# A two-layer model: layer 1's rotation table built in the dense layer, one bias product at the start, projection steps in another order

## The chip, the cores and the metric

The kernel runs on one core of a Trainium2 chip. The metric is the device time of one execution in microseconds (us), as the median of several runs. Engines are named TensorE (PE in the rows, PEld for its weight loads), VectorE (DVE), ScalarE (ACT), GpSimd (POOL) and SyncE (SP), which issues most of the transfers.

## What is computed

A model of two layers on 256 tokens of width 1024. Each layer projects the normed rows, runs a state space mixer, a latent attention and a sparse attention side by side, adds a cross attention, and ends with a feed-forward part: dense in layer 0, eight experts in layer 1.

```python
for l in range(DEPTH):
    proj = rmsnorm(h, mix_norm[l]) @ w_in[l]
    u, cq, ckv, kr, nq, nkv, ngate = jnp.split(proj, offsets, axis=-1)
    y_ssm = ssm_mixer(u, ...)
    y_mla = mla_mixer(cq, ckv, kr, ..., cos, sin)
    y_nsa = nsa_mixer(nq, nkv, ngate, ..., rel_bias)
    h = h + concatenate([rmsnorm(y_ssm), rmsnorm(y_mla), rmsnorm(y_nsa)]) @ w_out[l]
    h = h + cross_attn(h, mem, ...)
    hn = rmsnorm(h, ffn_norm[l])
    if l % 2 == 0:
        h = h + swiglu(hn, dense_w_gate, dense_w_up, dense_w_down)
    else:
        h = h + moe_swiglu(hn, moe_router, moe_w_gate, moe_w_up, moe_w_down)
return rmsnorm(h, final_norm)
```

In the state space mixer the state of each group turns in the complex plane from token to token: `ab_r, ab_i = mag * cos(li * dt), mag * sin(li * dt)`. The sparse attention adds a bias that depends on the distance of two tokens (`rel_bias`, 32 buckets by 6 heads). The compressed keys and values of the sparse attention pass through a small network with a GELU (`nsa_compress`).

## The kernel before

All five engines run programs written out by hand, with semaphores between them. **Weights** come as chunks of 128 x 2048 (1 MB) through a ring of six slots (`ring`), loaded by SP (L1150 to L1180) as TensorE frees them. Each chunk is split into two parts for products of full precision: ScalarE rounds it into an upper half (`layer_chunk_upper`, L457, into `colu` or `upper`), VectorE subtracts it from the chunk and leaves the lower half in place (`layer_chunk_lower`, L461). Each product of TensorE is three matmuls (`split_product`, L437 to L439): upper by upper, upper by lower, lower by upper. The left side is split in the same way (`colr`, `coll`). A layer has 27 common chunks; chunks 0 to 6 are the input projections, in the order u (0), zA (1), zB (2), q0 (3), q1 (4), ck and cv (5), vs (6).

**Results** of TensorE go through five banks in turn (`ROT`). Each tile has a name in a list of jobs and an engine that drains it; TensorE waits until the tile five places before is drained (`wait_free`), and for inputs by name (`wait_drained`).

**The start** (layer 0): ScalarE issues three small transfers (the one-hot table of distances, the bias table, the layer's columns), SP the rows x, the constants and the first chunks. TensorE makes the bias table of 6 heads in six products of 128 x 384 (L1272); ScalarE drains two of them (L1616) and VectorE four (L1897) into the place of `qz`; GpSimd writes all to memory (L2338) and reads them back skewed (L2369). VectorE computes the angles (`angles`), ScalarE the exponential and the sines (`trigonometry`); VectorE sums the squares of x (L1863), GpSimd takes the power (L2323), ScalarE scales the first half of the rows (L1601) and VectorE the second (L1889); TensorE transposes (L1202).

**The rotation table** `ftab` (in `big`, 2 x 8 x 256 columns) holds the powers of the unit rotation for all 256 tokens. GpSimd builds it in eight doublings of six tensor operations each (`double`, L2323). In layer 0 they stand beside the projections, all ahead of the power for the latent norms (`power(2, 4)`); in layer 1 also beside the projections, the last two doublings behind that power. The states (`states(0)`, first VectorE operation L1860 that reads `big`) and ScalarE's copy of the rotated key (L1707), whose place the doublings use as scratch, wait for it.

**VectorE in the projections**: lower half of chunk 4, squares of the latent columns (L1863), gates (L1977), rotation of the shared key (`rotate`), lower half of chunk 5, clearing and filling of `kc` and `qz` (L1998 to L2005), lower half of chunk 6, drains, the output parameters `cp` (L1860, L2026), the drain of `vs` (L2028), the lower half of the memory's columns (L2052), then states and query rotations. The GELU of the compressed tokens (L1720) stands on ScalarE behind the drains of queries, keys and values; TensorE's products of the result are L1376 to L1378.

**The dense layer** (`dense_pe`, `dense_act`, `dense_dve`) goes over 11 pieces of 256 columns; most of it is a loop with two pieces a turn. For each piece ScalarE copies the transposed units (L757), makes the upper halves of three chunks (L480) and takes the sigmoid product (L750); VectorE makes the remainders (L886, L486, L880). GpSimd has no part in it.

## Time and profile before

| | |
|---|---|
| time, median of 3 runs | 1760.9 us (1760.01 to 1760.96) |
| profiled execution | 1759.99 us, span 1758.2 us |
| TensorE busy | 1674.5 us (95%), mean granted clock 0.983 |
| VectorE busy | 1363.7 us (78%) |
| ScalarE busy | 1081.3 us (61%) |
| GpSimd busy | 225.8 us (13%) |
| layer 0: projections to cross attention | 0 to about 290 us |
| layer 0: dense layer | about 290 to 481 us |
| layer 1: projections to cross attention | about 481 to 770 us |
| layer 1: experts | about 770 us to the end |

A row of a timeline has the start in us from the span's start, the duration, the engine with the line of the kernel, the operation, what it writes and reads, shapes and count. In brackets stands how long the engine was idle before it, and which instruction of which engine ended that. A merged row (x4) lasts from the first start to the last end. A row of a table of stretches has, after the stretch and its length, the busy time and the number of instructions of each engine, then the mean granted clock of TensorE (1.00 is full, 0.50 half), the busy share of the transfer engines and what they moved. A row of waits has the engine and line that waited, who released it, the total in us, how many times, and the longest.

### The profile page before, as it was taken

Reading aid. Unit: us, or ns where it says so; the run is one execution under the profiler, and the core shown is the slowest. Engines: PE = TensorE matmul, PEld = TensorE weight load, DVE = VectorE, ACT = ScalarE, POOL = GpSimd, SP = SyncE. Lnnn points to the kernel's source line nnn. Section 1 sums busy time; section 2 is a strip of 40 time slices with the busy share of each in tenths; the row PEclk is TensorE's granted clock in tenths of the full one; section 3 lists DMA queues with packets and bytes.
Section 4 is the critical chain, followed back from the end, with each engine's and each line's share of the span. In section 5 each row is a group of like instructions: output and inputs, shape, how many; then the busy total and the mean of one; then the engine's idle time right before and its main releaser. Section 6 shows DMA issues by size and latency. Waiting matters only on the chain.

```text
span 1758.2 us, 24308 instructions
## 1 busy us (share of the span) xinstructions
PE 1674.5 (95%) x8490; PEld 1399.4 (80%) x8490; DVE 1363.7 (78%) x1508; ACT 1081.3 (61%) x1190; POOL 225.8 (13%) x236
## 2 busy tenths in 40 slices
PE   7799999999987999989999999999999999999995
PEld 6768888888785888878888888888888888888783
DVE  6876656545568756578898989998989999889895
ACT  4355454434353554447777777777777777777773
POOL 6534001000066420031000000000000000000200
PEclk9899999999999999989999999999999999999998
DMA  9402334955431124249999999999999999999992
GB/s 369 158 24 71 146 144 151 367 189 191 174 138 48 49 96 164 102 184 422 377 377 378 376 381 375 370 389 381 375 381 376 383 377 362 388 372 357 418 364 83
DMA packets 67610, 475.94 MB, mean 271 GB/s; under 512 B 7544, under 2 KB 7544, under 8 KB 12889
## 3 DMA queue, kind: packets, MB, share of 16 engines
q1 hardware_dynamic: 62016, 450.93, 66.9%
q0 software_dynamic: 5296, 24.04, 3.5%
q8 instruction: 39, 0.64, 0.1%
q10 hardware_dynamic: 232, 0.12, 0.1%
q14 instruction: 27, 0.21, 0.0%
HBM read 461.82 MB, written 13.24 MB: 270 GB/s over the span
## 4 chain that ended last, share of the span: by engine, by line
PE 82%; DVE 9%; ACT 4%; issue 3%; DMA 2%; POOL 1%; DVEq 0%; ACTq 0%; POOLq 0%; SPq 0%
PE bank L437 24%; PE bank L439 24%; PE bank L438 24%; DVE lower L461 2%; ACT upper L480 1%; PE bank L628 1%; DMA ring<-in_weights 1%; PE bank L1423 1%; ACT upper L457 1%; DVE xel L986 1%; PE bank L1521 1%; PE bank L1313 1%; PE bank L1422 1%; DVE row L1860 1%; PE bank L1202 1%
## 5 line engine op out<-in xcount | busy, mean ns | idle before, releaser
L486 DVE TENSOR_TENSOR lower<-ring,upper 128x2048 fp32r<-128x2048 f32 x369 | 845.6, 2292 | 145.8 <-ACT upper L480 132.8
L480 ACT ACTIVATE upper<-ring 128x2048 fp32r<-128x2048 f32 x369 | 706.3, 1915 | 111.3 <-PE bank L439 101.8
L437 PE MATMUL bank<-upper,xeu 128*128 128x512 f32 x896 | 359.8, 402 | 3.9 <-DVE lower L486 3.2
L439 PE MATMUL bank<-upper,xel 128*128 128x512 f32 x896 | 350.5, 391 | 0.0
L438 PE MATMUL bank<-lower,xeu 128*128 128x512 f32 x896 | 349.5, 390 | 0.0
L437 PE MATMUL bank<-upper,htu 128*128 128x512 f32 x536 | 209.7, 391 | 5.3 <-DVE htl L1002 3.8
L439 PE MATMUL bank<-upper,htl 128*128 128x512 f32 x536 | 208.7, 389 | 0.0
L438 PE MATMUL bank<-lower,htu 128*128 128x512 f32 x536 | 208.6, 389 | 0.0
L437 PEld LDWEIGHTS bank<-upper,xeu 128*128 128x128 f32 x896 | 168.3, 188 | 36.4 <-DVE lower L486 4.4
L439 PEld LDWEIGHTS bank<-upper,xel 128*128 128x128 f32 x896 | 168.2, 188 | 35.9
L438 PEld LDWEIGHTS bank<-lower,xeu 128*128 128x128 f32 x896 | 168.7, 188 | 31.7
L461 DVE TENSOR_TENSOR lower<-ring,upper 128x2048 fp32r<-128x2048 f32 x42 | 99.3, 2364 | 67.3 <-ACT upper L457 66.9
L437 PEld LDWEIGHTS bank<-upper,htu 128*128 128x128 f32 x536 | 100.6, 188 | 31.0 <-issue 9.7
L457 ACT ACTIVATE upper<-ring 128x2048 fp32r<-128x2048 f32 x42 | 80.3, 1912 | 60.5 <-PE bank L439 60.5
L439 PEld LDWEIGHTS bank<-upper,htl 128*128 128x128 f32 x536 | 100.6, 188 | 21.1
L438 PEld LDWEIGHTS bank<-lower,htu 128*128 128x128 f32 x536 | 100.6, 188 | 20.5
L439 PE MATMUL bank<-colr,lower 128*128 128x256 f32 x384 | 110.3, 287 | 0.0
L800 ACT ACTIVATE htu<-bank 128x256 fp32r<-128x256 f32 x112 | 43.4, 388 | 98.1 <-PE bank L628 97.8
L2323 POOL TENSOR_TENSOR small<-small,cst 128x2 f32<-128x2 f32 (+2 forms) x12 | 20.3, 1690 | 570.9 <-DVE small L1866 570.8
L437 PE MATMUL bank<-colr,upper 128*128 128x256 f32 x256 | 76.1, 297 | 11.2 <-DVE lower L461 9.4
L796 ACT ACTIVATE big<-bank 128x256 f32<-128x256 f32 x112 | 43.0, 384 | 65.8 <-PE bank L439 65.8
L439 PE MATMUL bank<-upper,coll 128*128 128x512 f32 (+1 forms) x208 | 77.7, 374 | 0.0
(376 smaller groups left out, 2574.8 us busy)
## 6 DMA issues: line engine op xcount, KB each, us to landing
ring<-in_weights SPq DMA_DIRECT2D x423, 1024.0 KB, 5.7
routed_rows<-g POOLq DMA_DIRECT2D x1, 4096.0 KB, 36.6
lp<-in_lparams POOLq DMA_DIRECT2D x1, 3634.5 KB, 14.2
lp<-in_lparams SPq DMA_DIRECT2D x1, 3584.0 KB, 13.6
memraw<-routed_rows POOLq DMA_DIRECT2D x7, 512.0 KB, 6.2
expert_rows<-xk POOLq DMA_DIRECT2D x7, 512.0 KB, 6.9
skewed_bias<-attn POOLq DMA_DIRECT2D x1, 1152.0 KB, 10.9
h<-in_x SPq DMA_DIRECT2D x1, 1024.0 KB, 5.3
```

The lines of the kernel that those rows point to most:

```text
L437: pe.matmul(to, x_up, w_up, start=start, stop=False, skip_group_check=True)
L438: pe.matmul(to, x_up, w_lo, start=False, stop=False, skip_group_check=True)
L439: return pe.matmul(to, x_lo, w_up, start=False, stop=stop, skip_group_check=True)
L457: act.activation(upper_slot(c), ring[:, c % RING, :], ACT.Copy).then_inc(wt_upper[l], 1)
L461: dve.tensor_tensor(lower[:, c % RING, :], ring[:, c % RING, :], f32(upper_slot(c)), ALU.subtract).then_inc(wt_split[l], 1)
L480: act.activation(upper[:, third(q), :], ring[:, q % RING, :], ACT.Copy).then_inc(done, 1)
L486: dve.tensor_tensor(lower[:, q % RING, :], ring[:, q % RING, :], f32(upper[:, third(q), :]), ALU.subtract).then_inc(done, 1)
L628: ins = pe.transpose(banks[2][:, f * P:(f + 1) * P], hr[:, i % 2, 0, f * P:(f + 1) * P], ident)
L796: act.activation(gs[:, i % 2, 0, :], banks[i % 2][:, 0:256], ACT.Silu).then_inc(m["silu"], 1)
L800: act.activation(htu[:, i % 2, 0:256], banks[2][:, 0:256], ACT.Copy).then_inc(m["ht_up"], 1)
L986: ins = dve.scalar_tensor_tensor(xel[buf][:, k, :], banks[5 + k // 4][:, (k % 4) * P:(k % 4 + 1) * P], cols[:, C_FFN + k:C_FFN + k + 1], f ...
L2323: return pool.tensor_tensor(out, a, b, op)
```

## The change

In the program's order:

- The columns are the first of ScalarE's three transfers. TensorE makes one bias product of 6 x 384 (heads by distances); VectorE drains it into one row per head (`biasrow`, in `vm`); SP writes it to memory 128 times over, between chunk 5 and chunk 6. ScalarE's first drain of `vm` waits for that write.
- In layer 0 ScalarE sums the squares of x, and VectorE scales both halves of the rows. Layer 1 keeps the old division.
- On VectorE, in both layers, the lower half of chunk 5 stands ahead of the gates, and the key's rotation behind the lower half of chunk 6.
- On ScalarE, in both layers, the GELU stands ahead of the drains of queries, keys and values.
- On GpSimd, in layer 0, the power for the latent norms stands ahead of the last doubling.
- Layer 1's step lengths, angles and sines are computed in the dense layer, around pieces 6 and 7, which are taken out of the loop. GpSimd builds layer 1's table there, into `col` and `row`, with scratch in `g` and `big`. When TensorE has done its last product of the layer, ScalarE copies the table to `big` (two copies of 2048 columns), ahead of its scaling of the rows.
- TensorE's wait for the split memory columns moves from before the loop over the heads to its first use in it (the second turn).

```diff
-        bias = attn[:, 2 * NH * T:2 * NH * T + NH * 384].rearrange("p (h n) -> p h n", h=NH)
-        biasrows = vm[0:33, :, :].rearrange("p t n -> p (t n)")
+        biasrow = vm[0:NH, 0, :]
...
@@ dense_act @@
-            with act.Fori(1, (DENSE_PIECES - 1) // 2 - 1) as r:
+            e = (DENSE_PIECES - 1) // 2 - 2
+            with act.Fori(1, e) as r:
                 step(0, 2 * r, r)
                 step(1, 2 * r + 1, r)
+            next_steps()
+            step(0, 2 * e, e)
+            next_trigonometry()
+            step(1, 2 * e + 1, e)
...
@@ dense_dve @@
+            next_angles()
+            step(0, 2 * e, e)
+            step(1, 2 * e + 1, e)
...
@@ block.sync @@
+            sp.wait_ge(p_dve, 2)
+            sp.dma_start(scratch[:, :, :], biasrow.unsqueeze(1).broadcast_to([NH, P, 384])).then_inc(s_scr, 16)
             load(RING, RING)
...
@@ block.tensor @@
-            pe.wait_ge(p_dve, 2)
-            for hh in range(NH):
-                mm(banks[2 + hh][:, 0:384], biasrows[:, hh * P:(hh + 1) * P], pt[0:33, 0, 0:384],
-                   start=True, stop=True).then_inc(p_pe, 1)
+            pe.wait_ge(p_dve, 1)
+            mm(banks[7][0:NH, 0:384], pt[0:33, 1, 0:NH], pt[0:33, 0, 0:384], start=True, stop=True).then_inc(p_pe, 1)
...
@@ block.scalar @@
+            act.dma_start(lp[:, 0:LP["cols"][1]], lparams[0][:, 0:LP["cols"][1]]).then_inc(cols_landed, 16)
             act.dma_start(pt[0:33, 0, :], onehot).then_inc(bias_landed, 16)
             act.dma_start(pt[0:33, 1, 0:NH], relb).then_inc(bias_landed, 16)
-            act.dma_start(lp[:, 0:LP["cols"][1]], lparams[0][:, 0:LP["cols"][1]]).then_inc(cols_landed, 16)
             act.wait_ge(cols_landed, 16)
             step_lengths(0)
-            bias_drain(0)
+            act.wait_ge(x_landed, 16)
+            for t in range(TT):
+                ins = A(xkf[:, t * D:(t + 1) * D], h[:, t, :], ACT.Square, accum_out=ss[:, t:t + 1])
+            ins.then_inc(p_act, 1)
             trigonometry(0)
-            bias_drain(1)
 
             for l in range(L):
                 if l:
-                    act.wait_ge(next_lp_landed, 16)
-                scale_rows(1)
-                if l:
-                    step_lengths(l)
+                    act.wait_ge(weights_used, RING + LAYER_CHUNKS)
+                    act.wait_ge(ftab_ready[l], 1)
+                    A(bigf[:, 2048:4096], rowf, ACT.Copy).then_inc(ftab_ready[l], 1)
+                    A(bigf[:, 0:2048], colf, ACT.Copy).then_inc(ftab_ready[l], 1)
+                    act.wait_ge(ftab_ready[l], 3)
+                    scale_rows(1)
                 else:
                     layer_chunk_upper(act, 0, 0)
...
@@ block.vector @@
+            angles(0)
             dve.wait_ge(bias_landed, 32)
...
             for l in range(L):
-                norm_h(xkf, l)
...
+                if l:
+                    norm_h(xkf, l)
+                    scale_rows(1)
+                else:
+                    dve.wait_ge(p_act, 1)
+                    mean_eps(0, 2, D).then_inc(ss_ready[l], 1)
+                    dve.wait_ge(rstd_ready[l], 1)
+                    for t in range(TT):
+                        dve.tensor_scalar(row[:, t, :], h[:, t, :], rstd[:, t:t + 1], None, ALU.mult).then_inc(row_ready[l], 1)
+                    dve.wait_ge(p_pe, 1)
+                    dve.tensor_copy(biasrow, banks[7][0:NH, 0:384]).then_inc(p_dve, 1)
...
@@ block.gpsimd @@
             for l in range(L):
                 pool.wait_ge(ss_ready[l], 1)
                 power(0, 2, rstd_ready[l])
                 if l == 0:
+                    tables(0, ftab[:, 0], ftab[:, 1], kTf[:, 512:])
+                    for m in (1, 2, 4, 8, 16, 32):
+                        link(double(m))
+                    pool.wait_ge(p_dve, 3)
                     power(6, 2, p_pool)
                     link(double(64))
-                    double(128).then_inc(ftab_ready[l], 1)
                 pool.wait_ge(ss_ready[l], 2)
                 power(2, 4, rstd_ready[l])
                 if l == 0:
+                    double(128).then_inc(ftab_ready[l], 1)
...
                     pool.wait_ge(next_lp_landed, 16)
+                    tables(1, *(f.rearrange("p (j n) -> p j n", j=8) for f in (colf, rowf)), bigf[:, 3072:4096])
+                    for m in (1, 2, 4, 8, 16, 32, 64):
+                        link(double(m))
+                    double(128).then_inc(ftab_ready[1], 1)
```

VectorE in the projections of a layer, from the means of the latent squares to the lower half of chunk 6. L461 (L462 after the change) is a lower half, L1860 (L1871) on `rt` is the rotation. Before:

```order
L1866 TENSOR_SCALAR small<-small 128x2 x2
L1977 TENSOR_SCALAR small<-small 128x36
L1978 MEMSET row 128x2x64
L1860 TENSOR_TENSOR rt<-row,cst 128x32 x2
L1860 TENSOR_TENSOR row<-rt 128x2x16
L1860 TENSOR_TENSOR rt<-row,cst 128x32 x2
L1860 TENSOR_TENSOR row<-rt 128x2x16
L461 TENSOR_TENSOR lower<-ring,upper 128x2048
L1998 MEMSET attn 128x2x256
```

And with the change:

```order
L1877 TENSOR_SCALAR small<-small 128x2 x2
L462 TENSOR_TENSOR lower<-ring,upper 128x2048
L1984 TENSOR_SCALAR small<-small 128x36
L1985 MEMSET row 128x2x64
L1998 MEMSET attn 128x2x256
L1999 COPY attn<-lp 128x2x16
L2000 MEMSET attn 64x768
L2001 MEMSET attn 64x768
L2004 COPY attn<-bank 64x512
L2005 COPY attn<-bank 64x512
L462 TENSOR_TENSOR lower<-ring,colu 128x2048
L1871 TENSOR_TENSOR rt<-row,cst 128x32 x2
```

The lower half of chunk 5 stands seven operations earlier, and the rotation behind the lower half of chunk 6.

GpSimd between the layers, from its last transfer of layer 0 to layer 1's first power (on `small`, 128x2) and the table. Before:

```order
L2400 DMA expert_rows<-g 16x1x64
L2323 TENSOR_TENSOR small<-small,cst 128x2
L2341 COPY big<-small 128x8
L2342 COPY big<-small 128x8
L2323 TENSOR_TENSOR big<-big 128x8
```

And with the change, the end of the table, whose first rows now follow the transfer directly:

```order
L2325 TENSOR_TENSOR col<-col 128x8x128
L2325 TENSOR_TENSOR g<-row 128x1024
L2325 TENSOR_TENSOR row<-col,row 128x8x128
L2325 TENSOR_TENSOR big<-row,col 128x1024
L2325 TENSOR_TENSOR col<-col,g 128x8x128
L2325 TENSOR_TENSOR row<-row,big 128x8x128
L2325 TENSOR_TENSOR small<-small,cst 128x2
L2325 TENSOR_TENSOR small<-small,cst 128x4
L2325 TENSOR_TENSOR lp<-g,big 128x512 x2
```

The whole table (two copies and 48 operations) stands ahead of layer 1's first power, and nothing of it is left between the powers and the states.

## Rows read from the trace of the kernel before

**Rows 1.** Waits of TensorE, 0 to 110 us

```profile
PE bank L1376 <- ACT hidr L1721: 2.5, 1, 2.5
```

**Rows 2.** Waits of TensorE, 478 to 620 us

```profile
PE bank L1202 <- ACT row L1601: 7.3, 1, 7.3
```

**Rows 3.** Timeline of the start, all engines

```profile
1.76 0.38 ACTq L1639 DMA_DIRECT2D lp<-in_lparams  x1
...
11.19 1.22 DVE L1863 CUSTOM_DVE_ANT_0 xk<-h 128x1024 f32<-128x1024 f32 x1
...
13.92 0.69 POOL L2323 TENSOR_TENSOR small<-small,cst 128x2 f32<-128x2 f32 x1 [13.47 <-DVE small L1866]
...
20.85 0.55 PE L437 MATMUL bank<-colr,colu 128*128 128x256 f32 x1 [1.27 <-DVE coll L1873]
```

**Rows 4.** Transfers issued from 0 to 40 us: count, size, median us to landing

```profile
skewed_bias<-attn POOLq DMA_DIRECT2D x1, 1152.0 KB, 10.9
h<-in_x SPq DMA_DIRECT2D x1, 1024.0 KB, 5.3
...
lp<-in_lparams ACTq DMA_DIRECT2D x1, 50.5 KB, 7.2
```

**Rows 5.** Busy time of each engine in stretches of both layers' starts

```profile
20.00:24.00 4.00, 3.15 (x15) 3.18 (x16) 4.00 (x9) 2.31 (x3) 3.60 (x15) 1.00 1.01 410
24.00:28.00 4.00, 4.00 (x34) 4.00 (x34) 3.81 (x6) 0.00 (x0) 3.98 (x3) 1.00 0.79 329
...
488.50:491.50 3.00, 3.00 (x15) 3.00 (x15) 1.07 (x3) 2.99 (x8) 0.00 (x0) 0.50 0.00 0
491.50:492.00 0.50, 0.50 (x5) 0.50 (x4) 0.50 (x2) 0.49 (x3) 0.00 (x0) 0.68 0.00 0
```

**Rows 6.** Timelines of VectorE and TensorE, layer 0's projections, 49 to 86 us

```profile
49.59 1.29 DVE L1977 TENSOR_SCALAR small<-small 128x36 f32<-128x36 f32 x1
...
58.65 4.43 DVE L461 TENSOR_TENSOR lower<-ring,upper 128x2048 fp32r<-128x2048 f32 x1
...
63.13 0.58 PE L437 MATMUL bank<-colr,upper 128*128 128x256 f32 x1 [9.37 <-DVE lower L461]
...
68.43 2.29 DVE L461 TENSOR_TENSOR lower<-ring,colu 128x2048 fp32r<-128x2048 f32 x1
...
75.52 0.42 DVE L2026 SCALAR_TENSOR_TENSOR cp<-cp,pt 128x256 f32<-128x256 f32 x1
...
77.12 0.27 PE L1326 MATMUL bank<-cst,row 128*128 128x128 f32 x1
...
83.52 1.13 PE L1313 MATMUL bank<-uT,lp 128*128 128x256 f32 x4
...
84.69 1.29 DVE L1860 TENSOR_TENSOR lp<-bank,big 128x512 f32<-128x512 f32 x2 [0.41 <-PE bank L1313]
```

**Rows 7.** The same two engines in layer 1's projections, 540 to 548 us

```profile
540.23 2.55 DVE L2026 SCALAR_TENSOR_TENSOR cp<-cp,pt 128x256 f32<-128x256 f32 x1
...
543.56 2.07 PE L1313 MATMUL bank<-uT,lp 128*128 128x256 f32 x4 [4.17 <-DVE vs L2028]
...
547.15 1.27 DVE L1860 TENSOR_TENSOR lp<-bank,big 128x512 f32<-128x512 f32 x2
```

**Rows 8.** Timeline of GpSimd: end of layer 0's table; start and end of layer 1's

```profile
60.89 4.41 POOL L2323 TENSOR_TENSOR big<-big,attn 128x1024 f32<-128x1024 f32 x1
...
497.64 0.20 POOL L2341 COPY big<-small 128x8 f32<-128x8 f32 x1 [10.73 <-ACT small L1625]
...
539.98 2.52 POOL L2323 TENSOR_TENSOR big<-big,attn 128x1024 f32<-128x1024 f32 x1
```

**Rows 9.** The dense layer: a stretch of it, and ScalarE's timeline in one piece

```profile
428.00:473.00 45.00, 45.00 (x206) 37.24 (x205) 20.76 (x16) 17.50 (x16) 0.00 (x0) 1.00 0.51 186
...
395.30 0.60 ACT L757 ACTIVATE htu<-bank 128x512 fp32r<-128x512 f32 x1 [4.04 <-PE bank L518]
395.79 1.91 ACT L480 ACTIVATE upper<-ring 128x2048 fp32r<-128x2048 f32 x1
```

More of the change, by code:

```diff
@@ L332, in trunk @@
         s_out = sem("s_out")
+        bias_back = sem("bias_back")
         mem_kept = sem("mem_kept")
@@ L902, in dense_dve @@
             step(1, 1)
-            with dve.Fori(1, (DENSE_PIECES - 1) // 2 - 1) as r:
+            e = (DENSE_PIECES - 1) // 2 - 2
+            with dve.Fori(1, e) as r:
                 step(0, 2 * r, r)
                 step(1, 2 * r + 1, r)
+            next_angles()
+            step(0, 2 * e, e)
+            step(1, 2 * e + 1, e)
             step(DENSE_PIECES - 3, DENSE_PIECES - 3)
@@ L1611, in transposes_upper @@
                     ins.then_inc(tr_upper[l], 1)
-            def bias_drain(hh):
-                act.wait_ge(p_pe, hh + 1)
-                A(bias[:, hh, :], banks[2 + hh][:, 0:384], ACT.Copy).then_inc(p_act, 1)
             def step_lengths(l):
@@ L1894, in _ @@
                 dve.memset(ap, v)
-            def bias_drain(hh):
-                dve.wait_ge(p_pe, hh + 1)
-                dve.tensor_copy(bias[:, hh, :], banks[2 + hh][:, 0:384]).then_inc(p_dve, 1)
             q = [par[:, i, :] for i in range(16)]
@@ L1946, in _ @@
                     mean_eps(6, 2, D).then_inc(p_dve, 1)
-                else:
-                    angles(l)
                 layer_chunk_lower(dve, l, 2)
@@ L2291, in _ @@
                 if l == 0:
-                    dense_dve(dve, last_half)
+                    dense_dve(dve, last_half, lambda: angles(1))
                 else:
@@ L2329, in _, with tables, double @@
             pool.wait_ge(cst_landed, 16)
+            table = {}
+            def tables(l, re, im, other):
+                table.update(re=re, im=im, other=other)
+                pool.wait_ge(trig_ready[l], 4)
+                pool.tensor_copy(re[:, :, 0:1], par[:, 8, :].unsqueeze(2))
+                link(pool.tensor_copy(im[:, :, 0:1], par[:, 7, :].unsqueeze(2)))
+            def double(m):
+                re, im = table["re"], table["im"]
+                a, b = (f[:, :, m - 1:m].broadcast_to([P, 8, m]) for f in (re, im))
+                x = gf[:, 0:8 * m].rearrange("p (j n) -> p j n", j=8)
+                y = table["other"][:, 0:8 * m].rearrange("p (j n) -> p j n", j=8)
+                tt(re[:, :, m:2 * m], re[:, :, 0:m], a, ALU.mult)
+                tt(x, im[:, :, 0:m], b, ALU.mult)
+                tt(im[:, :, m:2 * m], re[:, :, 0:m], b, ALU.mult)
+                link(tt(y, im[:, :, 0:m], a, ALU.mult))
+                tt(re[:, :, m:2 * m], re[:, :, m:2 * m], x, ALU.subtract)
+                return tt(im[:, :, m:2 * m], im[:, :, m:2 * m], y, ALU.add)
             for l in range(L):
@@ L2368, in _ @@
                     skew = bass.AP(scratch.tensor, 127, [[383, P], [P * 384, NH], [1, T]])
-                    pool.dma_start(btab[:, :, :], skew).then_inc(s_scr, 16)
-                else:
-                    link(double(64))
-                    double(128).then_inc(ftab_ready[l], 1)
+                    pool.dma_start(btab[:, :, :], skew).then_inc(bias_back, 16)
                 for j in range(8):
```

94 lines of the change are left out of this document (31 added, 63 removed).

## The prediction

> **What bounds the kernel now.** The profiled execution lasted 1759.99 us, with a span of 1758.2; the median of the runs is 1760.9, 0.9 above it. I read the page first: TensorE is busy 95% of the span, and its row of tenths is near 9 everywhere except at the start of each layer. So only time in which TensorE stands still or runs at its low clock can be won. I then asked for TensorE's waits in the two places where the change works, and for the timelines of the other engines around them.
>
> In layer 0, TensorE waits 9.37 us in one piece for VectorE's lower half of a weight chunk [rows 6], and 2.5 us for the GELU [rows 1]. The 2.5 us come again in layer 1, with an equal row. Where layer 1 begins it waits 7.3 us for the scaled rows [rows 2]. The start is a chain of landings and small steps: the first feature product stands at 20.85 us [rows 3]. VectorE and GpSimd hold each other up: the same L2026 took 0.42 us in layer 0, with GpSimd idle [rows 6], and 2.55 us in layer 1, while GpSimd was at the last steps of its table [rows 7, 8].
>
> **The change, part by part.**
>
> *Start.* The step sizes' columns are issued third on ScalarE's queue, at 1.76 us, and land 7.2 later, at 8.96; x, the first transfer of all, takes 5.3 and is there near 6 [rows 3, 4]. VectorE's angles stand between the columns and its squares of x at 11.19; GpSimd's power follows at 13.92 [rows 3]. Now the columns are issued first, at about 0.74. With the same 7.2 they land at 7.9. ScalarE squares x at once, at about 1.2 us for each half (VectorE's row has 1.22), so the power starts near 11.0, 2.9 sooner. Scaling both halves on VectorE costs some 0.3 more than one on each engine, but the first product waits for ScalarE's half of chunk 0, and ScalarE is free 3.2 sooner, since it neither drains bias products nor scales a row. I take **3.2 us**. If the columns land no sooner it is 2.2; if they take the 5.3 us of x, another 1.9 sooner, it is 5.1. The six bias products vanish into this; the single one runs before the rows are there. The bias write moves from GpSimd's queue to SP's, behind chunk 5 and ahead of chunk 6 and the big parameter load. Its reader, the skew load, is wanted only after 100 us, and chunk 6 only near 59, so I cost it at nothing; it would cost something if it held SP's transfers for over 20 us, against the 10.9 it took before [rows 4].
>
> The clock: 15 matmuls fit between 20 and 24 us and 34 in the next four, so TensorE went from its low level to its high one at about 24 us, some 3.3 us after the first product, although it had been busy with bias products and transposes before [rows 5]; the column of the granted clock prints 1.00 for both stretches, so here the counts are read. At the start of layer 1, the level rose in the half microsecond after 491.5, right behind three in which TensorE did 15 transposes at the low level [rows 5]. The Trainium skill's "TensorE: Matmul & The Clock Gate" (Part 4) says that transposes do not count as activity for the gate. The rows of layer 1 speak against it. By the page the rise stays 3.3 us behind the first product, as it was; by layer 1's rows it may come with the first product. I take no gain, and 1.2 us as its bound: 15 products at 0.21 us against 0.13, the pace at which VectorE hands over the columns.
>
> *Layer 0, chunk halves.* From 49.59 to 58.65 VectorE does the gates and the key rotation, slowed by GpSimd; then the lower half of chunk 5, 4.43 us where an undisturbed one takes 2.29 [rows 6]. TensorE had been ready at 63.13 - 9.37 = 53.76. Put ahead, that half is done between 51.9 and 54.0: the 9.4 us wait goes. What is late next is chunk 6. TensorE needs it after 48 products, 5.6 us later, at 59.4. VectorE has the gates (1.5) and the 5.3 us of clearing and copying that stand between the two halves now (63.1 to 68.43), so that half begins near 59.8 and ends at 62.1 to 64.2: a new wait of 2.7 to 4.8 us. The products of chunk 6 then end at 67.7 to 69.8, against 77.12 before, where L1326 follows them [rows 6]: 7.3 to 9.4 won. L1313 stood 6.4 us behind that point, at 83.52 [rows 6]. The rotation, copies, parameter products and the drain of "vs" behind it end near 73 at the latest, before L1313 wants that bank (74.1 at the earliest), and GpSimd's table, which ended at 65.3 [rows 8], starts over 3 us sooner. If the new wait drops the clock, up to 2 us are lost. I take **8.0**, with ends at 5.3 and 9.4.
>
> *GELU.* It is put ahead of the drains of the query and key products; its table load fits into ScalarE's idle time before them. TensorE's 2.5 us wait goes in both layers [rows 1]. The scores behind need VectorE's drain of "kcv" and its second scan, both done by then. **5.0 us**; should half of one wait come back elsewhere, 3.7.
>
> *Layer 1's table.* GpSimd ran it from 497.64 to 542.5 [rows 8], beside the projections. Without it VectorE runs as in layer 0 after 66 us. There the scan of the first state begins 1.17 us after TensorE's L1313 (83.52 to 84.69) [rows 6]; in layer 1 L1313 waited 4.17 and VectorE came 3.59 after it, at 547.15 [rows 7]. Without both it begins at 539.39 + 1.17 = 540.56: **6.6 us**. Bound: 5.0, if the rotation behind chunk 6 costs VectorE more. Then the clock: the four matmuls of L1313 took 2.07 us at the low level and 1.13 at the high one [rows 6, 7]; two such spells follow the waits in layer 1, so I take **1.0**, between 0 and 2.
>
> *Where the table goes.* In the dense layer TensorE is busy all of the 45 us from 428 to 473, VectorE 20.8, GpSimd not at all [rows 9]. ScalarE has 4.04 us idle ahead of each piece's copy [rows 9], which hides the added exponential and sines and their table loads, and the sigmoid's reload behind them delays nothing that TensorE needs within 5 us. The lower halves may be stretched by the 2.1 us seen above; they are ready some 6 us ahead of their use, an estimate from the order of the program and 5.6 us for each chunk's products. The table starts near 428 and takes 45 us at most, since VectorE was fuller beside it in layer 1: done by 473. ScalarE's two copies of 2048 columns (1.91 each [rows 9]) fit into the 7.3 us wait [rows 2]. Cost: nothing.
>
> Sum: 3.2 + 8.0 + 5.0 + 6.6 + 1.0 = 23.8. The profiled execution would take 1736.2, a median 1737.1. The stream of weights in the experts' part is paced by TensorE and moves with it.
>
> **Rivals.**
>
> *The wait moves instead of going (22%).* In layer 0 GpSimd's longest steps still stand beside VectorE. If the clearing, the copies and chunk 6 each meet them, that half ends at 67 rather than 63, and the clock drops too: 3 us of the 8.0 remain, 18.8 in all, **1742**. For it: everything that VectorE did from 49 to 65 was stretched [rows 6]. Against: fills and reads of PSUM were not.
>
> *More is won (12%).* The columns land early, TensorE never cools in layer 1, the start warms sooner: 5.1 + 9.4 + 5.0 + 6.6 + 2.0 + 1.2 = 29.3, **1732**.
>
> *The dense layer pays (6%).* Some eight lower halves fall beside the table. If TensorE felt 2.1 us of each, 17 us would be given back: **1754**. Against it: their lead of some 6 us.
>
> *Slower (3%).* GpSimd is starved in the dense layer and layer 1 starts late. The copies must end by 487, the table thus by 483; each microsecond beyond that is lost. It must take 45 + 10 us to cost anything, and over 45 + 10 + 23.8 + 3.5 = 82 us to make the kernel slower. At 90 us, 35 late: **1772**. VectorE is half idle there, so this is remote.
>
> *Nothing that can be told (3%).* Layer 0's gain and the start's fail, and dense and expert parts give back the rest: **1760**.
>
> **The numbers.** The forecast has 54%. The range must leave out 2 in 10: from 1730 to 1748 it takes in the forecast with its bounds (2.2 + 5.3 + 3.7 + 5.0 = 16.2, so 1744.7), the first two rivals, and no more. A measurement here tells 0.2%, about 3.5 us, from no change: faster 94%, within 3%, slower 3%.
>
> **What would show it.** First product near 17.6; no 9.4 us wait, one of 3 to 5 us at chunk 6; no wait for the GELU in either layer; L1313 of layer 1 without a wait; 0.42 us in place of 2.55 for the last parameter product; GpSimd's table in the dense layer, near 414 to 459, for 14 us are won ahead of it; TensorE still full there. I would be wrong if layer 0's wait stayed near 9, or if ScalarE's copies ended after GpSimd's power at the start of layer 1.

## The result, and the profile after

The changed kernel takes **1737.7 us** (median of 4 runs, 1735.67 to 1739.33), against 1760.5 for the kernel before in the same comparison: a ratio of 0.988, 95% interval 0.9861 to 0.9898. Faster by 1.2%, and 0.7 us from the forecast of 1737. The profiled execution took 1737.24 us, with a span of 1735.3, 22.9 less than before (the sum of the prediction's terms was 23.8).

| | before | after |
|---|---|---|
| span of the profiled execution | 1758.2 us | 1735.3 us |
| TensorE busy | 1674.5 us (95%) | 1664.6 us (96%) |
| first feature product | 20.85 us | 15.45 us |
| first transposes of the latents behind chunk 6, layer 0 | 77.12 us | 68.66 us |
| first scores of layer 0 | 108.99 us | 98.47 us |
| first transposes of layer 1 | 488.29 us | 477.86 us |
| first state's products of layer 1 | 543.56 us | 528.32 us |
| first scores of layer 1 | 573.64 us | 551.72 us |

Up to the first scores of layer 0, 10.5 us are won; from there to the start of layer 1 nothing (379.4 us now, 379.3 before); from there to layer 1's first scores 11.5; behind them 1.0. The terms had put 13.7 of the 23.8 into the first of these stretches (3.2 + 8.0 + 2.5) and 10.1 into layer 1. So the total hides two errors. TensorE's timeline at the places of [rows 2, 3, 6, 7]:

```profile
15.45 0.35 PE L438 MATMUL bank<-colr,colu 128*128 128x256 f32 x1 [0.78 <-DVE coll L1884]
...
60.62 0.58 PE L438 MATMUL bank<-colu,colr 128*128 128x256 f32 x1 [7.33 <-DVE lower L462]
...
68.66 0.27 PE L1334 MATMUL bank<-cst,row 128*128 128x128 f32 x1
...
75.05 1.13 PE L1321 MATMUL bank<-uT,lp 128*128 128x256 f32 x4
...
85.97 0.23 PE L1384 MATMUL bank<-hid,lp 64*64 64x16 f32 x1
...
477.86 3.65 PE L1214 MATMUL bank<-cst,row 128*128 128x128 f32 x16 [7.19 <-ACT row L1610]
...
528.32 1.13 PE L1321 MATMUL bank<-uT,lp 128*128 128x256 f32 x4
```

L1384 starts without a wait (before, 2.5 us for the GELU, [rows 1]), and so does L1321 in layer 1 (4.17, [rows 7]). But a wait of 7.33 us stands at the first product of chunk 6, where 2.7 to 4.8 had been forecast. It is put down to VectorE's lower half, L462. VectorE's and ScalarE's timelines ahead of it:

```profile
43.07 2.29 DVE L462 TENSOR_TENSOR lower<-ring,upper 128x2048 fp32r<-128x2048 f32 x1
...
50.49 0.69 DVE L2005 COPY attn<-bank 64x512 f32<-64x512 f32 x1
58.05 2.52 DVE L462 TENSOR_TENSOR lower<-ring,colu 128x2048 fp32r<-128x2048 f32 x1 [6.87 <-ACT colu L458]
```

```profile
56.11 1.91 ACT L458 ACTIVATE colu<-ring 128x2048 fp32r<-128x2048 f32 x1 [13.58 <-DMA ring<-in_weights]
```

VectorE had nothing to do for 6.87 us; ScalarE had waited 13.58 for chunk 6 itself, which landed near 56 us. The issues on SP's queue, and the transfers in stretches:

```profile
3.57 2.04 SPq L1164 DMA_DIRECT2D ring<-in_weights  x4
11.49 0.95 SPq L1177 DMA_DIRECT2D skewed_bias<-vm  x1
21.59 9.51 SPq L1164 DMA_DIRECT2D ring<-in_weights  x1
31.15 3.60 SPq L1179 DMA_DIRECT2D lp<-in_lparams  x1
```

```profile
20.00:25.00 5.00, 5.00 (x44) 5.00 (x43) 3.88 (x6) 2.40 (x2) 4.84 (x8) 1.00 0.93 383
25.00:33.00 8.00, 8.00 (x68) 7.87 (x66) 7.62 (x17) 2.40 (x2) 7.68 (x11) 1.00 0.43 78
33.00:43.00 10.00, 9.06 (x77) 8.99 (x77) 8.78 (x12) 8.36 (x9) 9.65 (x6) 1.00 0.96 307
...
56.00:60.00 4.00, 0.00 (x0) 0.00 (x0) 1.95 (x1) 3.88 (x6) 2.62 (x3) 0.50 0.66 282
60.00:68.00 8.00, 7.38 (x43) 7.38 (x44) 6.09 (x20) 2.26 (x7) 1.48 (x2) 0.65 0.77 286
```

The bias write is issued at 11.49, behind six chunks, and is at work from about 25 us. There the transfers fall from 383 to 78 GB/s and the engines that carry them are busy 43% of the time. The issue of chunk 6, at 21.59, is itself held for 9.51 us. TensorE's granted clock drops to 0.50 in the wait and averages 0.65 behind it. That is the changed kernel's open end.

In layer 1 and in the dense layer the forecast's rows came out as said: the last parameter product takes 0.42 us where it took 2.55 [rows 7], and GpSimd's table runs from 417.9 to 464.1, ahead of ScalarE's copies. (The timelines of VectorE, GpSimd and ScalarE.)

```profile
521.41 0.42 DVE L2028 SCALAR_TENSOR_TENSOR cp<-cp,pt 128x256 f32<-128x256 f32 x1
```

```profile
461.76 2.37 POOL L2325 TENSOR_TENSOR row<-row,big 128x1024 f32<-128x1024 f32 x1
475.76 0.71 POOL L2325 TENSOR_TENSOR small<-small,cst 128x2 f32<-128x2 f32 x1 [11.63 <-DVE small L1877]
```

```profile
470.70 1.91 ACT L1657 ACTIVATE big<-row 128x2048 f32<-128x2048 f32 x1 [3.02 <-PE bank L440]
472.52 1.89 ACT L1658 ACTIVATE big<-col 128x2048 f32<-128x2048 f32 x1
```

### The profile page after: what moved, and what is told of

Its sections match the earlier page's. It is cut to its first block, busy times and chain, and to the rows that moved or that the text cites. A ratio compares the mean times of both kernels' runs of the same rounds, so it can differ in the third digit from the quotient of the medians.

```text
span 1735.3 us, 24261 instructions
## 1 busy us (share of the span) xinstructions
PE 1664.6 (96%) x8480; PEld 1393.9 (80%) x8480; DVE 1348.1 (78%) x1501; ACT 1088.8 (63%) x1195; POOL 219.4 (13%) x235
## 4 chain that ended last, share of the span: by engine, by line
PE 85%; DVE 6%; ACT 3%; DMA 3%; issue 2%; POOL 0%; DVEq 0%; SPq 0%; POOLq 0%; ACTq 0%
PE bank L438 25%; PE bank L440 24%; PE bank L439 24%; DMA ring<-in_weights 3%; ACT upper L481 1%; PE bank L629 1%; PE bank L1431 1%; DVE lower L462 1%; ACT upper L458 1%; PE bank L1530 1%; DVE xel L996 1%; PE bank L1321 1%; PE bank L1430 1%; PE bank L1214 1%; PE bank L1357 1%
## 5 line engine op out<-in xcount | busy, mean ns | idle before, releaser
L438 PE MATMUL bank<-upper,xeu 128*128 128x512 f32 x896 | 359.8, 402 | 2.4 <-DVE lower L487 2.4
L438 PE MATMUL bank<-upper,htu 128*128 128x512 f32 x536 | 209.7, 391 | 6.1 <-DVE htl L1012 4.6
L438 PEld LDWEIGHTS bank<-upper,xeu 128*128 128x128 f32 x896 | 168.3, 188 | 34.8 <-DVE lower L487 3.5
L462 DVE TENSOR_TENSOR lower<-ring,upper 128x2048 fp32r<-128x2048 f32 x42 | 97.9, 2332 | 69.8 <-ACT upper L458 69.4
L438 PEld LDWEIGHTS bank<-upper,htu 128*128 128x128 f32 x536 | 100.6, 188 | 31.9 <-issue 9.8
L439 PE MATMUL bank<-lower,colr 128*128 128x512 f32 (+1 forms) x224 | 78.0, 348 | 0.0
L438 PE MATMUL bank<-colr,upper 128*128 128x256 f32 x256 | 74.8, 292 | 2.8 <-DVE xor L1884 1.8
```

What stands on the lines that cost most here:

```text
L438: pe.matmul(to, x_up, w_up, start=start, stop=False, skip_group_check=True)
L439: pe.matmul(to, x_up, w_lo, start=False, stop=False, skip_group_check=True)
L462: dve.tensor_tensor(lower[:, c % RING, :], ring[:, c % RING, :], f32(upper_slot(c)), ALU.subtract).then_inc(wt_split[l], 1)
```

## The experiments

Twelve kernels ran, four at a time on one chip beside the kernel before (medians 1758.2, 1760.7 and 1758.3 us in the three groups), each timed in 5 rounds; the second group ran on another chip than the first and the third, so across groups the ratios are safer than the medians. A ratio is always to the kernel before. Line numbers in rows are each kernel's own.

**First group: what holds chunk 6?**

*The changed kernel once more.*

> The changed kernel once more, as the measure for the three kernels beside it. Every theory: 0.988 of the kernel before, near 1737.5 us, with chunk 6 of layer 0 landing near 56 us and TensorE waiting 7.3 us for its lower half.

Measured: 1738.1 us, 0.9885 (0.9866 to 0.9904). The wait at chunk 6 was 6.5 us (its first product at 61.37), the first scores stood at 99.49. Below, "the repeat" is this run.

*The write behind layer 0's parameters, on the same queue.*

```diff
-            sp.wait_ge(p_dve, 2)
-            sp.dma_start(scratch[:, :, :], biasrow.unsqueeze(1).broadcast_to([NH, P, 384])).then_inc(s_scr, 16)
             load(RING, RING)
             sp.dma_start(lp[:, ncols:], lparams[0][:, ncols:]).then_inc(lp_landed, 16)
+            sp.wait_ge(p_dve, 2)
+            sp.dma_start(scratch[:, :, :], biasrow.unsqueeze(1).broadcast_to([NH, P, 384])).then_inc(s_scr, 16)
```

> The bias write keeps its queue (SP's) and its source (six partitions), but stands behind chunk 6 and layer 0's parameters. Theory Q (the write holds up what is queued behind it on SP's queue): chunk 6 lands before 35 us, the wait of 7.3 us at 60.62 is gone or under 3, TensorE no longer cools there, and some 6 to 9 us are won over the changed kernel: 1729 to 1732. The chunks behind the write are then late, but the first of them is wanted only near 75 us. Rival S (VectorE's serial work, as I predicted, would hold chunk 6's half anyway): the wait stays at 3 to 5 us and 2 to 4 us are won. Rival N (the write slows the DMA engines wherever it stands, and chunk 6 only shares their time): no more than 1 us is won.

Measured: 1740.3 us, 0.9891 (0.9871 to 0.991), 2.2 us above the repeat. On the wait theory Q was right and rival N wrong, on the time (no more than 1 us won) it was the other way round. ScalarE took chunk 6 at 46.93, held by TensorE and no longer by the transfer; the wait at chunk 6 was 1.87 us. TensorE's waits up to 112 us, and VectorE's timeline, show what came in its place:

```profile
PE bank L1366 <- DVE hid L2062: 2.8, 1, 2.8
PE bank L1375 <- DVE row L1871: 2.7, 1, 2.7
...
PE bank L438 <- DVE lower L462: 2.2, 2, 1.9
```

```profile
54.75 2.00 DVE L1871 TENSOR_TENSOR rt<-row,cst 128x32 f32<-128x32 f32 x2
56.79 2.31 DVE L1871 TENSOR_TENSOR row<-rt 128x32 f32<-128x32 f32 x1
59.14 2.42 DVE L1871 TENSOR_TENSOR rt<-row,cst 128x32 f32<-128x32 f32 x2
61.60 0.19 DVE L1871 TENSOR_TENSOR row<-rt 128x32 f32<-128x32 f32 x1
...
73.31 3.26 DVE L2054 SCALAR_TENSOR_TENSOR memr<-memraw,lp,colr 128x256 fp32r<-128x256 f32 x8 [5.59 <-DMA memory_columns<-memraw]
```

An earlier chunk 6 moves VectorE's rotation to 54.75, beside GpSimd's largest doublings, where it takes 7.0 us (1.1 in the changed kernel, at 60.49, with GpSimd done). Then VectorE waits 5.59 us for the store of the raw memory columns, which GpSimd issues behind its table, at 61.35. The drain of the hidden units, for which TensorE waits, is queued behind that wait.

*The write on GpSimd's queue.* The two lines go from SP to GpSimd, ahead of its table (`pool.wait_ge(p_dve, 2)` and the same transfer).

> The bias write goes back to GpSimd's queue, with the six partitions as its source. Theory Q: chunk 6 lands before 35 us, the wait at chunk 6 is under 3 us, 6 to 9 us are won over the changed kernel: 1729 to 1732. Rival E (it is the DMA engines that serve the six partitions' rows that are held, whatever the queue): chunk 6 has a share of its bytes on those engines, still lands after 45 us, and 0 to 3 us are won. If GpSimd must issue it, its table may begin up to 1 us later; that is hidden.

Measured: 1736.9 us, 0.9876 (0.9857 to 0.9896). ScalarE took chunk 6 at 48.00 and TensorE did not wait for it. The transfers moved 383 GB/s from 25 to 33 us, where they had moved 78: behind GpSimd's queue the write from six partitions does not hold up the others, and rival E falls. TensorE waited 3.6 us one step on, and the clock fell:

```profile
64.05 0.45 PE L1339 MATMUL bank<-cst,row 128*128 128x128 f32 x1 [3.56 <-DVE kslT L2010]
...
72.64 2.08 PE L1319 MATMUL bank<-uT,lp 128*128 128x256 f32 x4
```

The first state's products took 2.08 us against 1.13, and the mean clock from 68 to 76 us was 0.50. The first scores stood at 98.40.

*The write's source is 128 partitions.* Here the bias table holds rows of x, so its content is left out.

```diff
-            sp.dma_start(scratch[:, :, :], biasrow.unsqueeze(1).broadcast_to([NH, P, 384])).then_inc(s_scr, 16)
+            sp.dma_start(scratch.rearrange("h p n -> p h n"),
+                         h[:, 0, 0:384].unsqueeze(1).broadcast_to([P, NH, 384])).then_inc(s_scr, 16)
```

> The write stays where the change put it on SP's queue, with the same size and the same 1536 byte rows in memory, but takes its data from 128 partitions (rows of x) and not from six. So the bias table holds something else; nothing else is left out. Theory P (the source is at fault: six partitions feed few DMA engines at a time): the write takes some 3 us of the queue, chunk 6 lands before 35 us, and 6 to 9 us are won over the changed kernel. Rival Q (a write of many small rows is slow wherever it reads, so the place in the queue is at fault): chunk 6 lands at 45 us or later and under 3 us are won.

Measured: 1735.6 us, 0.9861 (0.9839 to 0.9883). The slices of the transfers stayed above 320 GB/s where they had fallen to some 50, and layer 0's parameters landed 16.5 us after their issue and not 35.0; ScalarE took chunk 6 at 48.82, held by TensorE. So theory P holds for the landing: the form of this write makes it slow, and its place in the queue decides who pays. What in the form does it stays open, since the edit changed two things at once: the source has 128 partitions and not six, and the outermost dimension of the transfer is 128 partitions and not 6 heads. In the changed kernel the transfer engines were busy for 0.35 of the time from 26 to 31 us, at 54 GB/s; of the 16 engines that the profile counts this is between five and six, an estimate that would fit either. Of the 6 to 9 us only 2.5 came. The rest was again taken by the next steps: 1.9 us for the drain of L2013 with the rotation at 54.70 to 61.8, and VectorE's wait for the memory store, 2.3. The first scores stood at 96.17, 2.3 to 3.3 us earlier.

**Second group: the rungs behind it, and two parts of the change undone.**

*The write behind the first twelve loads; the memory store issued by ScalarE.*

```diff
             for q in range(RING + 1, 2 * RING):
                 load(q, q)
+            sp.wait_ge(p_dve, 2)
+            sp.dma_start(scratch[:, :, :], biasrow.unsqueeze(1).broadcast_to([NH, P, 384])).then_inc(s_scr, 16)
...
                     for i in range(1, 4):
                         memory_drain(i)
+                    act.wait_ge(p_act, 7)
+                    act.dma_start(mem_cols, memrawf).then_inc(mem_kept, 16)
```

> Two queues changed over the changed kernel: the bias write stands behind the first twelve weight loads on SP's queue, and the store of the raw memory columns is issued by ScalarE right behind its drains (near 52.5 us) and not by GpSimd behind its table (61.3 with the write from 128 partitions). Theory L (a ladder: behind the late chunk 6 stand VectorE's rotation beside GpSimd, and then VectorE's wait for that store, 2.3 to 5.6 us in the three kernels of the first batch): VectorE has no wait for the store, the drain of the hidden units is 2 to 5 us earlier, TensorE keeps one wait of 2 to 3.5 us ahead of the transposes near 62, and the first scores stand near 94 to 96 us against 98.5: 1732 to 1735. Rival C (the clock gives it back: any wait of 2 us there cools TensorE, and the products to 76 us are slow): TensorE's wait remains and so does the time, within 1.5 us of the changed kernel.

Measured: 1744.6 us, 0.9913 (0.9895 to 0.993): slower than the changed kernel, for a reason that I had overlooked. GpSimd issues the skew load of the bias table ahead of its part of the states, and now waits there for the late write (its timeline); TensorE stands 8.4 us for the second state:

```profile
87.28 1.08 POOL L2372 DMA_DIRECT2D btab<-skewed_bias  x1 [26.29 <-DMA skewed_bias<-vm]
88.39 2.49 POOL L2327 TENSOR_TENSOR lp<-g,big 128x512 f32<-128x512 f32 x2
```

The part on the store held: no wait for the hidden units' drain was left. The time falls outside both what theory L and what rival C had said.

*The same, with the rotation behind the copies.* `rotate` moves behind VectorE's copies out of "q1" and "cv"; TensorE's jobs go from cqT, ckvT, kwT, hid to cqT, kwT, hid, ckvT, and ScalarE's drains with them.

> As write_last_store_early, and VectorE's key rotation (some 7 us beside GpSimd's table) moves behind the drains of the chunk 5 and 6 columns; TensorE takes the transposes of the weights' keys and the products of the hidden units ahead of the transposes that need the rotated key. Theory L: the wait near 62 us goes too (under 1 us), TensorE stays at its high clock from 53 to 76 us, the first scores stand near 90 to 93 us: 1728 to 1732. Rival M (GpSimd's table, which ends near 61, or the scans of the states then bound the stretch): the wait moves to the first state's scan or to the drains behind it, and at most 2 us are won over write_last_store_early.

Measured: 1743.9 us, 0.9903 (0.9887 to 0.9918), with the same stall, here 10.4 us, at the second state. No wait ahead of the latents' transposes was left and the clock was at 1.00 from 68 to 84 us. But 2.3 us of wait appeared at chunk 3 (37.77) and 3.4 at chunk 6: VectorE's steps had met longer steps of GpSimd.

*The GELU back behind the drains* (the two instructions and their wait moved back behind the drains of "vm").

> The changed kernel with the GELU put back behind the drains of the value products, in both layers. My theory: the wait of 2.5 us for the hidden units' rows is back in each layer, less what VectorE's late third scan (1.7 us in layer 0) took back: 3.5 to 5.0 us slower than the changed kernel, 1741 to 1743. Rival: the states' scans bound the stretch by now, and it costs under 2 us.

Measured: 1745.1 us, 0.9912 (0.9899 to 0.9925). TensorE's timeline in layer 0:

```profile
89.34 0.23 PE L1384 MATMUL bank<-hid,lp 64*64 64x16 f32 x1 [2.46 <-ACT hidr L1728]
...
89.88 1.63 PE L1321 MATMUL bank<-uT,lp 128*128 128x256 f32 x4
91.44 1.06 PE L1327 MATMUL bank<-g,cp 128*32 128x256 f32 x2
```

From the first state's products to the first scores it takes 27.3 us in both layers, against 23.4 in both layers of the changed kernel (repeat): 3.9 us for each GELU, 7.8 in all, where I expected 3.5 to 5.0 (the medians differ by 7.0 us, the ratios by 4.8). The wait is 2.46 of each 3.9. In layer 0 the rest is the lower clock behind it: from the third state's products to the transposes at L1398 it takes 3.4 us (89.88 to 93.28), against 2.0 in the repeat (87.53 to 89.57). In layer 1 the four matmuls right behind the wait took 1.13 us, as in the repeat; the next steps were slower (2.27 us for the transposes at L1398, against 1.51), and the sum was the same.

*Layer 1's table back beside its projections*, with the angles, the exponential and the sines, and without the copies.

> The changed kernel with layer 1's table put back beside its projections, and with it the angles, the exponential and the sines; no copies by ScalarE where layer 1 starts. My theory: TensorE again waits some 4 us for the drain behind chunk 6 in layer 1, the last parameter product takes 2.5 us again, and 6.6 to 8.3 us are lost: 1744 to 1746, with the dense layer unchanged by less than 0.5 us. Rival D (the dense layer pays for the table): part of it comes back there, and the loss is under 5 us. Rival R (the order of the chunk halves alone already frees VectorE in layer 1): the wait stays away, and the loss is under 3 us.

Measured: 1745.5 us, 0.992 (0.9906 to 0.9935). TensorE's waits from 466 to 600 us:

```profile
PE bank L1214 <- ACT row L1610: 7.3, 1, 7.3
PE bank L1341 <- DVE kslT L2010: 3.7, 1, 3.7
```

From layer 1's first transposes to its first scores it takes 82.5 us (559.22 less 476.71), against 74.0 in the repeat of the changed kernel: 8.5 us lost. The medians differ by 7.5 us, the ratios by 6.2. Rivals D and R fall: the wait is back, and the dense layer takes what it takes with the table in it. From the last wait ahead of it (L1557) to the only one at its end (L438 for `htl`) it is 208.3 us here (255.44 to 463.70), in the repeat (257.80 to 466.05) and in the kernel before (266.99 to 475.27).

**Third group: the ladder at once, the order of the halves, the start, the dense layer's room.**

*Write on GpSimd's queue, store on ScalarE's, rotation behind the copies.* The edits are those shown above.

> The bias write on GpSimd's queue (as in write_on_gpsimd_queue: it landed before GpSimd's table was done, so GpSimd never waited for it), the store of the memory columns on ScalarE's queue, and the rotation behind the copies with TensorE's order to match (as in rotation_behind_copies, where TensorE stood at its high clock from 68 to 84 us). Theory L: none of the three waits behind the late chunk is left; the first state's products stand near 68 to 70 us, the first scores at 90 to 94 us against 98.5: 1730 to 1734. Rival J (VectorE and GpSimd share time so irregularly in layer 0 that each order of the same work meets other stretched steps): a wait of 2 us or more stands somewhere between 25 and 60 us, as the 2.3 us at 37.8 in rotation_behind_copies, and the time is within 2 us of the changed kernel.

Measured: **1731.3 us, 0.9848 (0.983 to 0.9865)**: faster than both kernels, some 6.5 us below the changed one. TensorE's waits up to 112 us, behind those of the start, and its timeline:

```profile
PE bank L1373 <- DVE row L1871: 1.9, 1, 1.9
PE bank L1294 <- ACT memraw L1633: 1.5, 1, 1.5
PE bank L1409 <- ACT pc L1735: 1.2, 1, 1.2
```

```profile
59.63 0.27 PE L1332 MATMUL bank<-cst,row 128*128 128x128 f32 x1
...
66.07 1.03 PE L1319 MATMUL bank<-uT,lp 128*128 128x256 f32 x4
...
92.66 0.63 PE L1428 MATMUL bank<-attn 96*128 96x128 f32 x2
```

No wait at chunk 6, none ahead of the transposes; chunk 6's products end 9.0 us earlier than in the changed kernel, the first state's stand at 66.07 (75.05), the first scores at 92.66 (98.47), layer 1 begins at 471.80 (477.86). Rival J falls too: the longest wait between 25 and 60 us is the 1.5 us at L1294. Not every wait is gone: L1373 waits 1.9 us for VectorE at 75.19, behind the first state. The write takes as long as before, 41.7 us from its issue, but nobody queued behind it is wanted sooner.

*The rotation first again.*

```diff
+                rotate((krp[:, :, 64:80], krp[:, :, 80:96]), z[:, :, 320:336], z[:, :, 336:352], cos2, sin2,
+                       [P, 2, 16]).then_inc(rope_ready[l], 1)
+                layer_chunk_lower(dve, l, 5)
```

(behind the gates; both are taken out where the change had put them.)

> The changed kernel with the key rotation put back ahead of chunk 5's lower half, in both layers. My prediction's term: 8.0 us would be lost in layer 0. What the traces say now: chunk 6 lands near 56 us in any case, so TensorE waits some 7 us for chunk 5 and then 2 to 4 us more for chunk 6 where it now waits 7.3 once; the products of chunk 6 end 1 to 3 us later: 1739 to 1741. Layer 1, where the rotation takes 1.2 us with GpSimd idle, loses under 0.5 us.

Measured: 1736.8 us, 0.9878 (0.9861 to 0.9895): no difference from the changed kernel, where I had expected 1.3 to 3.3 us more and a wait for chunk 5 as well. VectorE's timeline shows why there is none; before, the same rotation ran from 51.05 to 58.73 [rows 6]:

```profile
43.61 0.22 DVE L1871 TENSOR_TENSOR rt<-row,cst 128x32 f32<-128x32 f32 x2
43.86 0.19 DVE L1871 TENSOR_TENSOR row<-rt 128x32 f32<-128x32 f32 x1
44.09 0.29 DVE L1871 TENSOR_TENSOR rt<-row,cst 128x32 f32<-128x32 f32 x2
44.42 0.19 DVE L1871 TENSOR_TENSOR row<-rt 128x32 f32<-128x32 f32 x1
44.53 2.28 DVE L462 TENSOR_TENSOR lower<-ring,upper 128x2048 fp32r<-128x2048 f32 x1
```

```profile
43.49 1.05 POOL L2325 TENSOR_TENSOR small<-small,cst 128x4 f32<-128x4 f32 x1 [0.57 <-DVE small L1877]
44.52 4.04 POOL L2325 TENSOR_TENSOR big<-big 128x1024 f32<-128x1024 f32 x1
```

It takes 1.0 us, not 7.7, since GpSimd is then at its power over 4 columns, which the change put ahead of the last doubling. That the power's new place is what made the room is read from these rows (without it the last doubling would have followed at 43 us); no run undid it alone. The order of the halves is worth nothing in this kernel.

*The columns third again* (the columns' transfer behind the two others on ScalarE's queue).

> The changed kernel with the parameter columns issued third on ScalarE's queue again. Theory: the columns land near 8.8 us and not at 3.8, the exponential and the angles come that much later, but the squares wait for x only until 6.3, behind the exponential; the first feature product goes from 15.45 to about 18 to 19 us: 2.5 to 3.5 us slower in the start, of which chunk 6's landing, which follows the first chunk's release, passes on all or nearly all: 1740 to 1742. Rival: chunk 6 is issued when chunk 0 is released but lands by the backlog behind the bias write; then the start's loss is swallowed by the wait at chunk 6 and under 1 us is seen in the total.

Measured: 1737.6 us, 0.9888 (0.987 to 0.9906): the rival. The columns landed after 7.0 us, not 3.1; the first product stood at 18.07, 2.6 later, and chunk 2's upper half 4.3 later (25.96). Chunk 6 still came to ScalarE at 55.56, TensorE's wait for it fell from 7.3 to 4.2 us, and the first latents' transposes stood at 69.52, 0.9 later than in the changed kernel and 0.2 earlier than in the repeat. So the 2.6 us at the first product are worth nothing in the time of this kernel, as long as chunk 6 lands near 56.

*The dense layer's table twice* (built a second time, with the same values).

> The changed kernel with layer 1's table computed twice in the dense layer, the same values again. My 'slower' rival priced this: 90 us of table, 35 us late, 1772. From the trace of the changed kernel: the table runs from 417.9 to 464.1, so a second one ends near 510; the copies by ScalarE take 3.8 more and the rows follow; TensorE starts layer 1 near 515 instead of 478: 36 to 38 us slower, 1773 to 1776. The dense layer itself should lose under 1 us, since TensorE did not feel the first table. Rival: VectorE beside the second table falls behind TensorE, which then waits in the dense layer or at the start of layer 1's chunks: over 1780.

Measured: 1767.3 us, 1.005 (1.0033 to 1.0066): slower than before. TensorE's timeline at the start of layer 1:

```profile
507.96 3.64 PE L1214 MATMUL bank<-cst,row 128*128 128x128 f32 x16 [36.27 <-ACT row L1610]
```

The second table ended at 502.8. Counted from layer 0's first scores (99.43 here, 98.47 in the changed kernel), GpSimd was done 37.7 us later and layer 1 began 29.1 later. So 8.6 us of room stand behind the table as the change has it. From there on each microsecond should cost one, since only ScalarE's copies and scaling stand between the table's end and layer 1 (5.2 us from 502.8 to 507.96); a second length was not tried. That less was lost than I expected is the second table's own speed: 37.6 us against 46.2 for the first. VectorE stood still for 29.9 us of it, which fits what the rotation showed of the two engines, though nothing separates it here.

## Why the prediction was right, and where only its total was

The total and the range held, but that the total came within 0.7 us was luck in part: layer 0's start, halves and GELU gave 3.2 us less than their terms, and everything from layer 1 on gave 2.4 more. By its steps:

- **Start, 3.2 us: too small.** The first product came 5.4 us earlier, the upper end of 5.1 passed. What I mis-sized most was the columns' landing, taken as 7.2 us with 5.3 as the bound; put first, they took 3.1, and 4.1 in the repeat. Either way they were there before x, for which ScalarE's squares then waited (until 6.30 and 6.45). With the columns third again 2.6 of the 5.4 us were lost; the other 2.8, for which I had 2.2, belong to the rest of the new start. Apart from this stands the clock: 17 products fit into the two microseconds from 15.5 in the changed kernel's profile, so TensorE was at its high level with the first product, right behind 16 transposes and one bias product. So the Trainium skill's rule on transposes ("TensorE: Matmul & The Clock Gate", Part 4), by which the rise would stay behind the feature products, does not agree with this row. But in the repeat, the same program, only 8 fit and the rise came some 3 us later, as the page would have it. The bound of 1.2 us was the right kind of term, and a little low: at chunk 2's upper half the two executions are 1.7 us apart, 0.25 of it already at the first product. It falls or not from one execution to the next, and chunk 6's landing hides it either way. The two rows, of the changed kernel and of its repeat:

```profile
15.50:17.50 2.00, 2.00 (x17) 1.99 (x17) 2.00 (x6) 1.86 (x2) 1.76 (x9) 1.00 0.99 410
```

```profile
15.50:17.50 2.00, 1.80 (x8) 1.83 (x9) 2.00 (x7) 2.00 (x2) 1.76 (x9) 1.00 1.05 434
```

- **Chunk halves, 8.0 us: wrong.** Behind the start and up to the latents' transposes only 1.7 us were won (8.46 less the 6.75 by which chunk 2's half already stood earlier; 2.4 in the repeat). Two steps failed. "I cost it at nothing", on the bias write: the price was worked out from the 10.9 us that the write took from 128 partitions [rows 4]. In its new form it held chunk 6 till 56 us, 34.5 after its issue. My condition for a cost (over 20 us) was right, and met; the size was not. And the wait of 9.4 us, whose end I put down to the new order, went for another reason: undone, the order gives the same time. The rotation had been slow by where it met GpSimd, and it now meets it at another place. By the rows that is the work of the power's new place; this step is argued, not tested.
- **The new wait at chunk 6**: forecast, for VectorE's serial work, as 2.7 to 4.8 us. It stood at the place, was 7.3 long, and VectorE was idle. With the write out of the way VectorE's work is what is late, but one step behind it: 3.6 us at the drains, as the 1.9 to 3.6 us of three kernels show. The foreseen cooling was there. So the rival of the wait that moves was right on the place and the clock, and had 3 us of the 8.0 left where 1.7 to 2.4 were; its cause, GpSimd's long steps beside VectorE, was not the one that held chunk 6. The total escaped it by what the start and layer 1 gave beyond their terms.
- **GELU, 5.0: too small.** Undone, it costs 3.9 us in each layer: I counted the waits and not the low clock behind them. In the change itself layer 0 got only 2.1 for it (from the first state's products to the first scores 23.4 us against 25.5), since there, before, the product behind the wait had not been slow:

```profile
97.50 1.13 PE L1313 MATMUL bank<-uT,lp 128*128 128x256 f32 x4
```

- **Layer 1's table, 6.6 plus 1.0: right.** Undone, 8.5 us in the trace. In the change layer 1 won 11.5 up to its scores, where the terms had 10.1.
- **Dense layer, nothing: right**, to 0.1 us (208.3 with the table and without). VectorE's lower halves were stretched to 3.54 us there without TensorE feeling it. The rival on the other side was priced right in its kind: room of 8.6 us where I had 10, and slower than before with a second table (1767.3, for which it had 1772).

So 13.7 forecast for start, halves and layer 0's GELU came out as 10.5, and 10.1 as 12.5 from there on. What stays open: the parts do not add. The GELU (7.8) and the table (8.5) undone leave some 6.6 for the rest of the change, of which columns and halves, undone one at a time, show nothing; for the columns it is chunk 6's landing that hides them. The power's new place, the single bias product and ScalarE's squares were never undone alone. Nor was it tried what the order of the halves is worth with chunk 6 on time.

## What to carry to other kernels

When a transfer is moved to another queue, price it in its new form (source and order of its dimensions) and count everything issued behind it until it is through; a profile of the old form says little. When one wait is removed, walk down the same engine's queue for the next thing that lands or is drained late: here 6.5 us appeared only when three had gone together (bias write, memory store, rotation). The write alone, in three forms, gave from 2.5 us to none; store and rotation were never moved without it. A step that is slow beside another engine is not fixed by its place in its own order, but by what the other engine does at that time: look at that before giving the reorder the credit.

## What the runs showed of the hardware that I had not expected

- A write of 1152 KB out of six partitions, in rows of 1536 bytes, held SP's queue and brought all transfers down to a mean of 78 GB/s for 8 us (25 to 33 us; 54 from 26 to 31), against 383 just before; the same size out of 128 partitions, with the partitions as outermost dimension, left them above 320 GB/s. On GpSimd's queue the write from six partitions took 39.9 us to land and left the transfers at 383 GB/s. An issue behind it on SP's queue was itself held for 9.51 us.
- The same six VectorE operations on 128x32 elements (the rotation) took 1.0 us beside GpSimd's power over 4 columns and 5.8 to 8.7 beside its operations on 128x1024 elements, which take 1.9 us or more each. GpSimd pays too: the first of these took 4.04 us beside VectorE's lower half.
- The same wait of 2.46 us of TensorE cost 2.1 us in one place and 3.9 in another, by whether the clock fell behind it (1.13 or 1.63 us for the next four matmuls in layer 0; in layer 1 of the same kernel they took 1.13, the clock fell just behind them, and the loss was again 3.9).
- The rise of TensorE's clock at the start of one program came with the first product in one execution and some 3 us later in another, 1.7 us apart at chunk 2's upper half (21.68 and 23.36).
